# Later layers of a two-block network: separate banks for value tiles, two branch outputs moved into the head steps, output tiles in pairs, late transfers on GpSimd

## The reference, cut to what matters

```python
for l in range(2):
    mod = (cond @ w_ada[l] + b_ada[l]).reshape(b, 6, d)
    sh_a, sc_a, gt_a, sh_f, sc_f, gt_f = [mod[:, i, None, :] for i in range(6)]
    u = rms_norm_2(x, g_mix[l]) * (1 + sc_a) + sh_a
    proj = u @ w_in[l]      # fox q,k,v | forget | mla latents | rope key | stick-breaking q,k,v | 3 gates
    ...
    y_fox = merge_heads_2(fox_attention(fq, fk, fv, log_f))            # 8 heads of 64
    cq = rms_norm_2(mla_ql, g_mla_q[l]);   q = to_heads(cq @ w_mla_uq[l], MLA_HEADS)
    ckv = rms_norm_2(mla_kvl, g_mla_kv[l]); kv = to_heads(ckv @ w_mla_ukv[l], MLA_HEADS)
    y_mla = merge_heads_2(mla_attention(q_nope, q_rope, k_nope, k_rope, mla_v))   # 8 heads
    y_sb = merge_heads_2(stick_breaking_attention(sq, sk, sv))         # 8 heads
    g = jax.nn.sigmoid(gate_logit).reshape(b, s, N_BRANCH, d)
    merged = g[:, :, 0] * (y_fox @ w_o_fox[l]) + g[:, :, 1] * (y_mla @ w_o_mla[l]) + g[:, :, 2] * (y_sb @ w_o_sb[l])
    x = x + gt_a * (merged @ w_out[l])
    u = rms_norm_2(x, g_ffn[l]) * (1 + sc_f) + sh_f
    h = jax.nn.silu(u @ w_ffn_gate[l]) * (u @ w_ffn_up[l])
    x = x + gt_f * (h @ w_ffn_down[l])
```

## Time and profile before

| | us |
|---|---|
| median of 3 runs (lowest to highest) | 2024.37 (2021.93 to 2025.31) |
| span of the profiled execution | 2024.1 |
| PE busy, share of the span | 1982.0, 98% |
| DVE busy | 1508.9, 75% |
| ACT busy | 1115.3, 55% |
| POOL busy | 202.0, 10% |
| mean granted TensorE clock | 0.992 |

### The profile page before, as it was taken

The page is one execution under the profiler, slowest core; times in us unless marked ns, Lnnn a source line. Parts: engine busy times, 40 slices in busy tenths (PEclk is TensorE's granted clock), DMA queues, the critical chain, the costliest instruction groups (busy, mean ns, idle before and its releaser), DMA issues.

```text
span 2024.1 us, 39780 instructions
## 1 busy us (share of the span) xinstructions
PE 1982.0 (98%) x13320; PEld 1815.8 (90%) x13320; DVE 1508.9 (75%) x3594; ACT 1115.3 (55%) x2304; POOL 202.0 (10%) x208
## 2 busy tenths in 40 slices
PE   8999999999999999999999999999999999999998
PEld 7769999999888899999998899989989889999997
DVE  5766697888778888888866577788886557777665
ACT  3243665998444444444565566554456466655444
POOL 0000398665000000000000000000000000000000
PEclk9999999999999999999999999999999999999998
DMA  8344654444765687777645433477764543345552
GB/s 310 130 136 146 228 174 171 148 143 134 251 254 196 223 302 284 280 281 283 233 148 177 165 115 105 161 246 240 246 230 157 177 157 115 115 159 185 186 181 100
DMA packets 109454, 388.23 MB, mean 192 GB/s; under 512 B 12160, under 2 KB 16528, under 8 KB 108304
## 3 DMA queue, kind: packets, MB, share of 16 engines
q1 hardware_dynamic: 95040, 335.40, 48.0%
q10 hardware_dynamic: 14288, 51.25, 7.2%
HBM read 379.76 MB, written 6.82 MB: 191 GB/s over the span
## 4 chain that ended last, share of the span: by engine, by line
PE 82%; DVE 6%; issue 5%; POOL 3%; ACT 2%; DVEq 2%; ACTq 0%; DMA 0%; POOLq 0%
PE bank L831 14%; PE bank L839 13%; PE bank L836 13%; PE bank L881 8%; PE bank L884 7%; PE bank L887 7%; POOL part_lo L1782 3%; PE bank L633 3%; PE bank L949 3%; PE bank L788 1%; DVE part_lo L2247 1%; PE bank L1075 1%; PE bank L1119 1%; PE bank L1158 1%; PE bank L664 1%
## 5 line engine op out<-in xcount | busy, mean ns | idle before, releaser
L1347 ACT ACTIVATE part_hi<-ring 128x512 fp32r<-128x512 f32 x1096 | 676.7, 628 | 399.9 <-PE bank L836 229.5
L1909 DVE TENSOR_TENSOR part_lo<-ring,part_hi 128x512 fp32r<-128x512 f32 x722 | 480.4, 688 | 163.3 <-ACT part_hi L1347 153.8
L831 PE MATMUL bank<-u_hi,part_hi 128*128 128x256 f32 (+1 forms) x1840 | 529.3, 288 | 5.1 <-POOL part_lo L1782 3.4
L839 PE MATMUL bank<-u_hi,part_lo 128*128 128x256 f32 (+1 forms) x1840 | 516.1, 280 | 0.0
L836 PE MATMUL bank<-u_lo,part_hi 128*128 128x256 f32 (+1 forms) x1840 | 514.7, 280 | 0.0
L831 PEld LDWEIGHTS bank<-u_hi,part_hi 128*128 128x128 f32 (+1 forms) x1840 | 345.2, 188 | 13.7 <-POOL part_lo L1782 4.6
L836 PEld LDWEIGHTS bank<-u_lo,part_hi 128*128 128x128 f32 (+1 forms) x1840 | 345.6, 188 | 3.0
L839 PEld LDWEIGHTS bank<-u_hi,part_lo 128*128 128x128 f32 (+1 forms) x1840 | 347.5, 189 | 0.0
L2247 DVE TENSOR_TENSOR part_lo<-ring,part_hi 128x512 fp32r<-128x512 f32 x300 | 204.2, 688 | 93.6 <-ACT part_hi L1347 87.6
L881 PE MATMUL bank<-part_hi,w_hi 128*128 128x512 f32 x688 | 269.1, 391 | 0.4 <-DVE w_lo L2114 0.2
L884 PE MATMUL bank<-part_hi,w_lo 128*128 128x512 f32 x688 | 268.0, 390 | 0.0
(11 more groups left out here) (302 smaller groups left out, 3011.7 us busy)
## 6 DMA issues: line engine op xcount, KB each, us to landing
ring<-stream_dram SPq DMA_DIRECT2D x606, 512.0 KB, 3.3
arena<-ada_dram ACTq DMA_DIRECT2D x96, 512.0 KB, 4.5
acts_kept<-act SPq DMA_DIRECT2D x32, 128.0 KB, 3.5
arena<-acts_kept SPq DMA_DIRECT2D x4, 1024.0 KB, 5.4
xT<-x_dram SPq DMA_DIRECT2D x4, 256.0 KB, 5.5
arena<-mem_dram SPq DMA_DIRECT2D x1, 1024.0 KB, 9.2
arena<-keys_dram SPq DMA_DIRECT2D x1, 1024.0 KB, 7.6
x_kept<-xT SPq DMA_DIRECT2D x1, 1024.0 KB, 10.0
```

The costliest lines, as they stand in the source:

```text
L831: m = pe.matmul(o, hi, u(cc), start=first, stop=False)
L839: m = pe.matmul(o, lo, u(cc), start=False, stop=last)
L1347: act.activation(part_hi[:, h % 4, 0:width], ring[:, n % RING, (h % 2) * width:(h % 2 + 1) * width], ACT.Copy).then_inc(hi_ready, 1)
L1909: v.tensor_tensor(part_lo[:, h % 4, :], ring[:, n % RING, (h % 2) * 512:(h % 2 + 1) * 512], part_hi[:, h % 4, :], ALU.subtract).then_inc(l ...
```

## The change

In both later layers:

- FV and SV/UV get banks of their own: FV and UV write banks 4 and 5, SV writes 6 and 7. They wait for no eviction, and of the tiles after them the first two wait for the eviction of the third tile before instead of that of the tile before (`evicted_before`).
- Branch output 0 is computed at head step 24, output 1 after step 26, into banks 0 and 1, once their bank's gate tile is evicted and (already at the first) the fox pairs are taken. Outputs 2 and 3 wait only for all pairs, the rest as before. The weight halves LH_WO + 1 and + 2 are made by ACT and DVE at head steps 23 and 24 instead of after the last step.
- Output tiles use four banks, 4 to 7. Tiles 0 and 1 are computed together: chunks 0 to 5 of each, then chunks 6 and 7 of each. ACT and DVE make the halves LH_OUT + 1 and + 2 before the last two chunks of `merged`, and LH_OUT + 3 after them.
- In the first of the two layers GpSimd, not ACT, issues the condition and all 24 slabs. It starts when PE has finished the last output tile.

```diff
+BANK_FV, BANK_SV, BANK_UV = 4, 6, 4
+AFTER_TOKENS = (LT_SQK, LT_UQ, LT_GATE)
+def wo_bank(jj):
+    return jj if jj < 2 else 4 + jj % 2
+def evicted_before(t):
+    if any(t - first in (0, 1) for first in AFTER_TOKENS):
+        return t - 3
+    return t - 1
...
-                    if c == 0:
-                        pe.wait_ge(tile_out, more + t) if (t or not isinstance(more, int)) else None
...
+                def layer_bank(t):
+                    pe.wait_ge(tile_out, tiles + (T_LAYER + evicted_before(t)))
+                    return bank[(T_LAYER + t) % 2]
...
-                def project_tokens(n, t):
-                    pe.wait_ge(tile_out, tiles + (T_LAYER + t))
+                def project_tokens(n, b0):
...
+                def branch_out_ahead(jj):
+                    pe.wait_ge(tile_out, tiles + (T_LAYER + LT_GATE + NUNIT - 1 + jj))
+                    pe.wait_ge(out_taken, l * (NUNIT // 2) + (8 + LAST_FOX // 2 + 1))
+                    branch_out(jj)
-                for s in range(NUNIT + 4):
+                for s in range(NUNIT + 3):
...
+                    if s == NUNIT:
+                        branch_out_ahead(0)
+                branch_out_ahead(1)
                 pe.wait_ge(out_taken, l * (NUNIT // 2) + (8 + NUNIT // 2))
-                for jj in range(24):
+                for jj in range(2, 24):
+                    if jj >= 4:
+                        pe.wait_ge(mix_taken, mixed + (M_OUT1 + jj - 1))
                     branch_out(jj)
...
+                pe.wait_ge(mix_taken, mixed + (M_OUT1 + 23))
+                out_chunks(0, range(0, 4), 1)
+                out_chunks(0, range(4, 6), 1)
+                out_chunks(1, range(0, 4))
+                out_chunks(1, range(4, 6))
+                out_chunks(0, range(6, 8)).then_inc(mix_full, 1)
+                out_chunks(1, range(6, 8), 2).then_inc(mix_full, 1)
+                for j in range(2, 8):
+                    if j >= 4:
+                        pe.wait_ge(mix_taken, mixed + (M_OUT1 + 24 + j - 3))
+                    out_halves(j, (0, 1)).then_inc(mix_full, 1)
+                    if j == 2:
+                        square_chunk(0, W_FFN)
+                    square_chunk(j - 1, W_FFN)
...
         @block.scalar
-                    if s + 1 < NUNIT:
-                        weight_high(LH_GATE + 2 * s + 3)
+                    if s <= NUNIT:
+                        weight_high(LH_GATE + 2 * s + (3 if s < NUNIT else 2))
...
-                weight_high(LH_WO + 1)
-                weight_high(LH_WO + 2)
                 act.drain()
                 gate_pair(0)
                 gate_pair(1)
...
                 weight_high(LH_OUT)
+                weight_high(LH_OUT + 1)
+                weight_high(LH_OUT + 2)
                 merged_high(6)
-                weight_high(LH_OUT + 1)
                 merged_high(7)
+                weight_high(LH_OUT + 3)
...
-                if l == 0:
-                    act.dma_start(cond[:, :], cond_kept).then_inc(cond_back, 16)
-                    for n, slab in enumerate((2, 3, 4, 5, 0, 1)):
-                        fetch_last(slab, n)
...
-                        if l == 0:
-                            act.wait_ge(ada_used, it * 2 + (NLAYER * ADA - ADA_EARLY - ADA_LAST + 1 + 4 + r - 3))
-                            fetch_last(r - 2, it * 2 + (4 + r - 2))
...
         @block.gpsimd
+            def late_modulations():
+                used = NLAYER * ADA - ADA_EARLY - ADA_LAST + 1
+                pool.wait_ge(mix_full, M_OUT1 + L_MIX)
+                pool.dma_start(cond[:, :], cond_kept).then_inc(cond_again, 16)
+                for n, slab in enumerate((2, 3, 4, 5, 0, 1)):
+                    fetch_last(slab, n)
+                with pool.Fori(0, (FT - 2) // 2 - 1) as it:
+                    for r in range(2):
+                        pool.wait_ge(ada_used, it * 2 + (used + 5 + r))
+                        fetch_last(r, it * 2 + (6 + r))
...
         @block.vector
-                    if s + 1 < NUNIT:
-                        weight_low(LH_GATE + 2 * s + 3)
+                    if s <= NUNIT:
+                        weight_low(LH_GATE + 2 * s + (3 if s < NUNIT else 2))
...
-                weight_low(LH_WO + 1)
                 for jj in range(24):
-                    weight_low(LH_WO + jj + 2)
+                    if jj:
+                        weight_low(LH_WO + jj + 2)
...
+                weight_low(LH_OUT + 2)
                 merged_low(DC - 2)
                 merged_low(DC - 1)
+                weight_low(LH_OUT + 3)
...
-                for j in range(8):
+                for j in range(1, 8):
                     weight_low(LH_OUT + 2 * j + 2)
-                    if j:
-                        add_out(j - 1)
+                    add_out(j - 1)
...
-                    v.wait_ge(cond_back, 32)
+                    v.wait_ge(cond_again, 16)
```

More of the change, by code:

```diff
@@ L429, in build @@
         plo_chunk = sem("mixed_normed_low_chunk_ready")
+        last_loaded = [sem(f"ada_last{i}_loaded") for i in range(6)]
         ada_used = sem("ada_used")
@@ L638, in linear, with tokens_major @@
                 return m
-            def tokens_major(n, t, src, kc, per, width, uses=0, more=0):
+            def tokens_major(n, b0, src, kc, per, width, uses=0):
                 for c in range(kc):
@@ L1088, in _ @@
                     m.then_inc(tile_full, 1)
[L1089 removed]
+                tokens_major(S_LAYER + L_UV, BANK_UV, kvlT, 2, 1, 512, uses)
                 pe.wait_ge(rows_set, l + 1)
@@ new lines, in out_chunks @@
+                def out_chunks(j, chunks, begun=0):
+                    for c in chunks:
+                        h = LH_OUT + 2 * j + c // 4
+                        pe.wait_ge(lo_ready, before + (h + 1))
+                        pe.wait_ge(mlo_chunk, l * DC + (c + 1))
+                        o = bank[4 + j][:, 0:S]
+                        hi, lo = (p[:, h % 4, c % 4 * P:(c % 4 + 1) * P] for p in (part_hi, part_lo))
+                        m = pe.matmul(o, hi, m_hi[:, c, :], start=c == 0, stop=False)
+                        if c == 0:
+                            m.then_inc(slot_begun, 1)
+                        m = pe.matmul(o, hi, m_lo[:, c, :], start=False, stop=False)
+                        if c == chunks[0] and begun:
+                            m.then_inc(half_begun, begun)
+                        m = pe.matmul(o, lo, m_hi[:, c, :], start=False, stop=c == DC - 1)
+                    return m
```

97 lines of the change are left out of this document (47 added, 50 removed).

## The result

| | us |
|---|---|
| kernel before, median of 4 runs (lowest to highest) | 2024.84 (2021.93 to 2025.46) |
| changed kernel, median of 4 runs (lowest to highest) | 2009.88 (2009.13 to 2011.72) |
| ratio, 95% interval | 0.993 (0.9918 to 0.9942) |
| span of the profiled execution, before and after | 2024.1, 2007.7 |

The change wins 15 us by the medians (12 to 17 by the interval) and 16.5 by the two traced spans; forecast were 15.4. To see where, the span is cut at the same events in both traces: the first projection matmul, the first gate matmul, product 2, the add of output tile 0, the first feed-forward matmul, the third tile of the feed-forward on DVE (its first operation on the finished gate tile, the COPY of L2459, after the change L2526; the refills of slabs begin behind it), the 22nd likewise, and the next layer's first projection.

What follows compares the result with a forecast made beforehand. PE was busy for 98% of the span, so each stage was priced by the engine that ends it: 9.8 + 1.4 + 0.4 + 3.8 = 15.4 off 2024.1 gave 2008.7, plus 0.3 for the runs' median: 2009.0, range 2004.0 to 2014.0.

Steps and rivals of the forecast that it cites:

- Part 1: Value tiles on banks of their own: PE's idle at five places per layer goes, 9.8 us, bounds 7.5 and 10.3.
- the hidden 0.16: At the value tiles, each of ten PE waits hides another 0.16 beyond the idle shown, 1.6 us in all.
- Part 2: Two branch outputs in the head steps: DVE's chain sets the pace; 1.3 us in the first layer, 0.1 in the second.
- The later pair: Head steps: with output 0 queued ahead of the last transposing and value products, the last pair is taken 1.1 us later.
- the 1.23 of the first layer: Before product 2: the first layer's loss from PE's lower clock behind its wait, 1.23 us, comes back.
- Part 3: Output tiles side by side: 0.2 us gained per layer, bounds 0 and 1.0; what tile 1 wins is given back.
- The ring: Output tiles: add, square and f_hi on ACT, its next half, DVE's half, next add; adds stay 3.53 us apart.
- Part 4: Transfers by GpSimd: 2.85 us at the first layer's feed-forward start and 1.0 in the loop, sum 3.8, bounds 0 and 5.
- No wait, or 0.1: Feed-forward start, first layer: DVE's wait for its first slab, which arrives between 1325.1 and 1327.3 and is wanted at 1327.2.
- the first rival: Feed-forward start: GpSimd's transfers are late, up to 3 us per issue; the sum loses 2.9, giving 2011.9; chance 0.14.
- It does not do what it says: Rival: value-tile places wait for something else as late, 2 us or less there, other parts halved; 2020.5 or more; chance 0.05.
- DVE is no bound: Rival, branch and output stages: PE's own waits count, 7.1 us in place of 1.8, giving 2003.7; chance 0.11.

Runs made afterwards that it cites:

- e5: Changed kernel with product written over its gate, next weight half between product and add, and one of two drains removed: 2006.08 us against 2024.45 of the kernel before.
- e1: Kernel before with only the value tiles on banks of their own: 2013.42 us against 2024.82, ratio 0.9945.
- e2: Kernel before with only the late transfers issued by GpSimd: 2021.55 us against 2024.82, ratio 0.9983.
- e4: Kernel before with only output tiles 0 and 1 side by side: 2024.65 us against 2024.82, ratio 1.0.
- e12: Changed kernel with lighter products, ACT's output halves ahead of its input, earlier GpSimd release, two modulations among output tiles, and halves LH_WO + 3 ahead of the sigmoids: 1997.09 us.
- e3: Kernel before with only two branch outputs moved inside the last head steps: 2022.86 us against 2024.82, ratio 0.9990.
- e8: Changed kernel with GpSimd issuing only the first seven late transfers and ACT the loop's refills again: 2011.42 us against 2024.45 of the kernel before.

## Why the prediction was right, point by point

- **Part 1** (forecast 9.8, bounds 7.5 to 10.3): alone it shortened its stretch by 5.54 + 5.17 = 10.7, in the changed kernel by 10.3. No new wait came in the place of the five. The addition to PE's visible idle (the hidden 0.16 and the slower restart) was needed: 7.5 would have been 3 short. Both sizes lie at or above my upper bound. The clock hides a little more: in the first layer of the changed kernel it was still at 0.61 in the mean from 1028 to 1030 us, inside this stretch, and before at 1.00.
- **Part 2** (1.3 and 0.1): 1.54 and 0.31. The later pair cost 0.87, not 1.1, which is the difference. That DVE's chain sets the pace is shown by e5. One step was surer than its evidence: I let the new order bring back the 1.23 of the first layer. In e1 it came back without part 2 (5.79 in both layers), and in e2 the second layer had it (7.00 from the last pair to product 2). Behind PE's wait of 1.82 the clock fell in three of the eight layers traced without part 2 (the first of the kernel before and of e4, the second of e2). With part 2 the wait is 0.40, and it fell there in none of 20 layers; the last pair to product 2 takes 4.6 in all of them, in e12 3.6. The order itself gains 0.3 to 0.4 per layer (121.4 against 121.7 to 121.8 where the clock did not fall); the other 1.2 of the first layer is there only where the clock would have fallen.
- **Part 3** (0.2 per layer): it cost 0.1 per layer. The ring is right; the step that failed is "tile 0 ends where it ended before, or 0.2 earlier". DVE's idle of 1.01 in front of add 0, released by PE, takes the place of its 1.00 for a half. PE waits 0.53 for LH_OUT + 2 between the first chunks of tile 0 and those of tile 1, and the add of tile 0 comes 3.2 us behind that wait, where I had 2.8 for PE.
- **Part 4** (2.85 and 1.0): 1.9 and 1.66. The 2.85 was itself the value of one execution: with the same code ACT's issues held its halves back by 2.29, 2.32 and 2.08 in e1, e3 and e4, and against these three the changed kernel wins 1.4 at the start and not 1.9. "No wait, or 0.1" for the first slab was wrong: 0.82. The term that was mis-sized is the landing: I took 4.7 for it. GpSimd was released at 1314.77, the slab was wanted 7.2 later (forecast: 7.5) and issued 0.76 later (bounds: 0.7 to 2.9), but it was there only 8.0 later, so it was under way for 7.2. The trace of before had told it: its slabs took up to 11.3 with seven in flight, and in e8 the six took 8.8 to 15.7, median 11.8. The median of all 24 was the wrong row to take. In the loop the forecast was too low by 0.7: that PE shows no wait there did not mean that ACT's issues cost nothing (e8).
- **The skill's rule.** GpSimd's 24 slab issues took 527 to 539 ns in the changed kernel and 527 to 541 in the others, with DVE busy for 84 to 88% of that time. So the starved transfer of some 3.1 us that the Trainium skill describes (SBUF — State Buffer, the section "A bandwidth-pool intuition that's wrong (but worth ruling out)" and the box "The 'DVE blocks DMA' trap (SWDGE)" ahead of it) is not seen here, and the price of 2.9 of the first rival was never paid in that way. These runs hardly test the rule, though. By the Trainium skill (SBUF — State Buffer, "Who interferes with whom") copy, cast and tensor_scalar can take both ports and tensor_tensor has no such mode. Beside the issues DVE ran mostly tensor_tensor and scalar_tensor_tensor, and of the three named only copies of one column.
- **The signs.** The waits for ACT's evictions went, the products stayed 9.06 apart per six and the adds 3.5, and ACT's halves followed the table at once. From the first projection to the last pair the layers got 4.0 and 4.5 shorter, not 4.9: there I had left out the later pair. PE waited only before output 3 and not before output 4. DVE did wait for a slab, which I had named as a sign of being wrong, and it is one: the start of part 4 was priced too high.
- **The rivals.** None came true, but two of their prices were off: by its own terms (part 1 at 2, the rest halved) "It does not do what it says" makes 2019.6 and not 2020.5, and the 2003.7 of "DVE is no bound" lies just outside the range that was said to hold most of it.
- **The time.** That 2009.0 came so near 2009.88 is in part luck. The span was forecast as 2008.7 and was 2007.7. The median of the runs lies 2.2 above that span, where I added the 0.3 of the kernel before. The two misses, 1.0 and 1.9, have opposite signs.
- **The sum.** 17.4 by stretches, of which 15.4 in stretches that the change touches. That this equals the forecast's 15.4 is luck too, by offsetting misses: part 1 + 0.5, part 2 + 0.45, part 3 - 0.65, part 4 - 0.3. The rest lies in unchanged stages, and the clock of PE differs there:

```profile
1026.00:1028.00 2.00, 2.00 (x17) 2.00 (x17) 1.83 (x5) 1.18 (x4) 0.00 (x0) 0.89 0.00 0
```

```profile
1026.00:1028.00 2.00, 2.00 (x12) 2.00 (x11) 1.82 (x6) 1.31 (x3) 0.00 (x0) 0.50 0.00 0
```

These are windows of before and of after (length, busy time of PE, its weight loads, DVE, ACT and POOL, granted clock, DMA share, GB/s) over the end of the sums ahead of the first later layer's projections. After has 0.50, the lower level of 1.2 GHz, where before had 0.89 in the mean, and starts its projections 0.92 later. Ahead of the second layer's projections it is the other way round: before has 0.50 in the last two us, after is back at 1.00 when they start.

## What to carry to other kernels

Price a stage by the engine that ends it, and a removed wait of PE by its idle plus the restart; PE's list of waits alone gave 3.4 us and more for two early tiles that were worth 2. When an edit yields nothing because a ring hides it, break the ring first and measure it again: part 3 went from 0 to 1.2 us per layer. Cheap orders (a half ahead of an input, a half between a product and its drain) were worth as much as moving whole tiles. And a stretch of one traced execution can be off by 0.5 to 1.2 us with the same code, by how a transfer lands or where the clock falls: take it from several traces before an edit is credited with it.

## What was not expected of the hardware

- A transfer of 512 KB with six others issued behind it by GpSimd within 3.4 us landed 4.0 and 4.1 us after its issue in two kernels, after 5.2 to 5.3 in three and after 7.2 and 7.6 in two. With two issued behind it, beside the output tiles, it took 3.7 to 4.0 in all three kernels. To issue alone what is waited for first may be worth trying; no run here does it.
- ACT's own issues are 0.345 each, yet in the loop they left idle time of 0.3 in front of its next half in 16 or 17 of 18 cases, up to 0.5, and stretched the loop by 1.65 to 1.9 us.
- Two drains of DVE around a dependent add, together with the order around them, cost at least 0.55 us per six outputs (four of which have an add) against one drain behind a longer operation; then PE became the bound.
- Behind the same wait of PE of 1.82 us the granted clock fell in some kernels and not in others: in the first layer of the kernel before and of e4, in the second of e2, in neither of e1.
